# Two blocks of hybrid layers on one core: summed GLA scores, state products in alternating row halves, and a later start for GpSimd's low parts

## What is computed

```python
# first kind, twice: hybrid mixer (MLA, MOBA, retention), then a squared-ReLU MLP
x = x + hybrid_mixer(rms_norm(x, attn_norm[l]), ...)
h = rms_norm(x, mlp_norm[l])
x = x + square(relu(h @ w_mlp_up[l])) @ w_mlp_down[l]      # 1024 -> 4096 -> 1024
# second kind, twice: gated linear attention (GLA) and grouped attention side by side,
# then a gated FFN and a gated embedding
scores = where(mask, einsum(q_dec, k_intra), 0)            # per direction, chunks of 64
o = scores @ v  +  q_dec @ state
state = state * exp(last) + k_state^T @ v                  # per head, 128 x 256
o_gla = rms_norm(o_forward + o_backward)
```

## Time and profile before

| | |
|---|---|
| median of three runs | 2049.84 us |
| the profiled execution | 2049.88 us, its span 2048.1 us |
| TensorE busy, matmuls (PE) | 1942.0 us, 95% |
| VectorE busy (DVE) | 1242.6 us, 61% |
| ScalarE busy (ACT) | 998.8 us, 49% |
| GpSimd busy (POOL) | 165.7 us, 8% |
| DMA | mean 154 GB/s |

### The profile page before, as it was taken

The page is one execution under the profiler, slowest core; times in us unless marked ns, Lnnn a source line. Parts: engine busy times, 40 slices in busy tenths (PEclk is TensorE's granted clock), DMA queues, the critical chain, the costliest instruction groups (busy, mean ns, idle before and its releaser), DMA issues.

```text
span 2048.1 us, 24920 instructions
## 1 busy us (share of the span) xinstructions
PE 1942.0 (95%) x9157; PEld 1582.7 (77%) x9157; DVE 1242.6 (61%) x2017; ACT 998.8 (49%) x1510; POOL 165.7 (8%) x68
## 2 busy tenths in 40 slices
PE   7899989999999989999999999999889999999996
PEld 6777878888777778887777787888767777878885
DVE  6756664547756674546668566665575685666645
ACT  5445544444445544444543745554446347454543
POOL 0000038300000038400000000000000000000000
PEclk9999999999999999999999999999989999999998
DMA  6443555555444554554533344646434343545562
GB/s 225 126 132 114 175 165 164 185 185 179 138 124 116 182 176 152 183 178 139 179 130 106 119 148 150 193 150 216 154 117 143 119 124 124 164 151 181 178 201 72
DMA packets 167328, 315.20 MB, mean 154 GB/s; under 512 B 12180, under 2 KB 20070, under 8 KB 167080
## 3 DMA queue, kind: packets, MB, share of 16 engines
q1 hardware_dynamic: 166612, 311.87, 48.3%
q10 hardware_dynamic: 596, 1.73, 0.2%
HBM read 312.51 MB, written 1.05 MB: 153 GB/s over the span
## 4 chain that ended last, share of the span: by engine, by line
PE 85%; DVE 8%; ACT 3%; issue 2%; DMA 0%; ACTq 0%; DVEq 0%
PE acc L541 73%; PE mix L513 4%; PE mix L569 2%; DVE lo L1264 1%; PE mix L550 1%; PE mix L770 1%; PE mix L699 1%; ACT junk L988 1%; PE mix L741 1%; PE mix L737 1%; PE mix L728 1%; DVE x L1347 1%; ACT hi L944 1%; PE mix L760 1%; PE mix L557 0%
## 5 line engine op out<-in xcount | busy, mean ns | idle before, releaser
L944 ACT ACTIVATE hi<-raw 128x1024 fp32r<-128x1024 f32 x600 | 634.6, 1061 | 649.3 <-PE acc L541 606.7
L1264 DVE TENSOR_TENSOR lo<-raw,hi 128x1024 fp32r<-128x1024 f32 x536 | 646.7, 1225 | 240.4 <-ACT hi L944 225.4
L541 PE MATMUL acc<-hi,xTh 128*128 128x512 f32 (+3 forms) x1760 | 704.0, 400 | 31.7 <-DVE xTl L1294 11.9
L541 PE MATMUL acc<-lo,xTh 128*128 128x512 f32 (+3 forms) x1760 | 686.2, 390 | 0.0
L541 PE MATMUL acc<-hi,xTl 128*128 128x512 f32 (+3 forms) x1760 | 686.0, 390 | 0.0
L541 PEld LDWEIGHTS acc<-hi,xTh 128*128 128x128 f32 x1760 | 339.8, 193 | 111.8 <-issue 31.4
L541 PEld LDWEIGHTS acc<-hi,xTl 128*128 128x128 f32 x1760 | 339.2, 193 | 68.2
L541 PEld LDWEIGHTS acc<-lo,xTh 128*128 128x128 f32 x1760 | 340.7, 194 | 61.7
L917 POOL TENSOR_TENSOR lo<-raw,hi 128x1024 fp32r<-128x1024 f32 x64 | 165.5, 2611 | 677.8 <-ACT hi L944 677.8
L541 PE MATMUL acc<-hi,hTh 128*128 128x512 f32 x432 | 171.8, 398 | 0.0
L541 PE MATMUL acc<-hi,hTl 128*128 128x512 f32 x432 | 171.2, 396 | 0.0
(11 more groups left out here) (208 smaller groups left out, 1673.6 us busy)
## 6 DMA issues: line engine op xcount, KB each, us to landing
raw<-in_w_in SPq DMA_DIRECT2D x200, 512.0 KB, 3.6
raw<-in_w_ffn_in SPq DMA_DIRECT2D x80, 512.0 KB, 4.5
raw<-in_w_mlp_up SPq DMA_DIRECT2D x64, 512.0 KB, 3.6
raw<-in_w_mlp_down SPq DMA_DIRECT2D x64, 512.0 KB, 4.2
raw<-in_w_ffn_out SPq DMA_DIRECT2D x44, 512.0 KB, 4.4
raw<-in_w_out SPq DMA_DIRECT2D x32, 512.0 KB, 4.2
raw<-in_w_o_gla SPq DMA_DIRECT2D x16, 512.0 KB, 3.6
raw<-in_w_o_attn SPq DMA_DIRECT2D x16, 512.0 KB, 3.7
```

Of the source, the lines that this page charges most:

```text
L541: last = nc.tensor.matmul(out, a[:, t * P:(t + 1) * P], w[:, slot, part, 0:c.n], start=(k == 0 and a is ah and w is L.hi), stop=(k == c.k_ ...
L944: nc.scalar.activation(L.hi[:, slot], L.raw[:, slot], ACT.Copy).then_inc(*n.up("hi_ready"))
L1264: v.tensor_tensor(L.lo[:, slot], L.raw[:, slot], L.hi[:, slot].bitcast(F32), ALU.subtract).then_inc(*n.up("low_by_dve"))
```

## The change

Three edits, and the table of signal totals that goes with them. First, VectorE adds the two masked scores of a head, and TensorE makes one product with the values where there were two. Second, the six state products of a head are issued in pairs from two banks, one in partitions 0 to 63 and one in 64 to 127; the waits for both banks of a pair come ahead of it. Third, GpSimd writes `lo` for `up` chunks from `to` = 8 on only. With them, VectorE advances its stream by one unit between `head_roots` and the last `head_rope`, and by one more ahead of the wait for the GLA squares.

```diff
@@ Plan.__init__
-            by = "low_by_pool" if c.name == "up" else "low_by_dve"
+            by = "low_by_pool" if c.name == "up" and c.to >= 8 else "low_by_dve"
@@ gla_head, on TensorE
-            for i, pairs in enumerate(KV_BANKS):
-                def kv(b):
-                    for m, (d, c) in enumerate(pairs):
+            for first in (0, 2):
+                two = [L.banks.get((ln, "gla", "kv", h, i)) for i in (first, first + 1)]
+                for b, use in two:
+                    pe.wait_ge(*n.at(f"bank{b}_drained", use))
+                for m in range(len(KV_BANKS[first])):
+                    for (b, use), pairs in zip(two, KV_BANKS[first:first + 2]):
+                        d, c = pairs[m]
                         r = slice(GLA_CHUNK * (c % 2), GLA_CHUNK * (c % 2 + 1))
-                        yield nc.tensor.matmul(L.mix[:, b, m * GLA_V:(m + 1) * GLA_V], L.ks[r, d, c // 2, h * P:(h + 1) * P], gv(r, c // 2), **f32)
-                fill(("gla", "kv", h, i), kv)
+                        last = nc.tensor.matmul(L.mix[:, b, m * GLA_V:(m + 1) * GLA_V], L.ks[r, d, c // 2, h * P:(h + 1) * P], gv(r, c // 2), **f32)
+                        if m == len(pairs) - 1:
+                            last.then_inc(*n.up(f"bank{b}_filled"))
...
-                    for d in range(2):
-                        yield nc.tensor.matmul(o, L.seenT[:, h % 2, d, t, :], gv(slice(0, P), t), start=(d == 0), stop=False)
+                    yield nc.tensor.matmul(o, L.seenT[:, h % 2, 0, t, :], gv(slice(0, P), t), start=True, stop=False)
@@ second_layer, on VectorE
             drain(last, key)
+            link(v.tensor_tensor(L.seenT[:, h % 2, 0], L.seenT[:, h % 2, 0], L.seenT[:, h % 2, 1], ALU.add))
             gla_states(h)
...
         head_roots()
+        s.on(1)
         for t in range(NT):
             head_rope(8, 10, t)
         tell("params_free")
         tell("tmp_free")
         tell("rows_ready")
-        s.to(44)
+        s.to(45)
```

More of the change, by code:

```diff
@@ L205 @@
     'glu_ready'           : [18, 0, 0],
-    'dve_step'            : [400, 0, 0],
+    'dve_step'            : [408, 0, 0],
     'params_loaded'       : [8, 0, 0],
@@ L225 @@
     'scale_ready'         : [2, 0, 0],
-    'low_by_pool'         : [64, 0, 0],
-    'low_by_dve'          : [536, 0, 0],
+    'low_by_pool'         : [48, 0, 0],
+    'low_by_dve'          : [552, 0, 0],
     'ones_ready'          : [2, 0, 0],
```

## The result

The changed kernel takes 2021.74 us (median of four runs, 2020.30 to 2022.62), the kernel before 2049.22 (four runs, 2048.13 to 2050.93). The ratio is 0.9867, interval 0.9855 to 0.9879: 27.5 us faster, where the forecast of 2021 meant 28.8. The profiled execution took 2020.30 us, its span 2018.5.

A forecast was written before the change was run, and what follows sets the result against it. TensorE, busy 95% of the span, was taken as the bound; 2049.9 - 15.1 - 10.0 - 4.4 = 2020.4, with 0.4 for `rows_ready` 2020.8, said as 2021. Forecast 2016 to 2025 (0.73), range 2014 to 2030 (some 0.87).

The forecast's parts named there:

- Place one: Ahead of local unit 80, both layers of the first kind: TensorE's waits for `xTl` go whole, -15.1 us (7.74 + 7.40).
- Rival (d): Norm's long tiny operations have another cause than GpSimd; place one costs 4.5 us more a layer, 2044.5 us; chance 0.03.
- The forecast of the eight low parts: Low parts moved to VectorE around the norm, 1.22 us each, delay no unit; smallest slack 0.7 us; at worst 9.8 a layer.
- rival (a): One moved low part comes late after all, the 0.7 us slack being thin; 2024 to 2031 us; chance 0.12.
- Place two: Ahead of local unit 45, both layers of the second kind: TensorE's wait for `lo` goes, -10.0 us (5.50 + 4.50).
- The feared wait for `rows_ready`: Behind local unit 45, the later turning makes TensorE wait 0.0 to 0.2 us at worst; 0.4 allowed in all.
- The sum of the scores: One product with the values per tile in heads 0 to 3: -2.2 us a layer, -4.4 over two layers.
- Its +0.12 there: Head 3: VectorE's added sum lengthens TensorE's existing wait for a low part by 0.12 us a layer.
- The alternating products: State products in eight heads: already run in pairs, so alternating the banks wins 0; ends +8 and -2 us.
- Rival (b): Alternating spoils the state products' pairs, as each pair waits for both banks first; 2029 us (+8); chance 0.05.
- (c): The old order of state products was strict and the pairs are new; 2011 us (-10); chance 0.03.
- Rival (e): VectorE is the bound in these stretches, so added operations lengthen the path by 23.1 us; 2073 us; chance 0.04.

The follow-up runs named there:

- Experiment 7: Changed kernel with GpSimd again writing the low parts of local units 80 to 83 of the first kind: 2035.79 us, ratio 0.9933.
- Experiment 8: Kernel before, GpSimd untouched, with the norm behind the second split instead of ahead of it: 2035.65 us, ratio 0.9933.
- experiment 5: Changed kernel with each bank's wait right ahead of its first state product, products still alternating: 2021.68 us in a single run.
- experiment 4: Kernel before with the alternating order of the state products alone: 2047.95 us, ratio 0.9993.
- experiment 6: Kernel before with all state products of partitions 0 to 63 first, then all of 64 to 127: 2050.99 us in a single run.
- experiment 10: Changed kernel with the old state-product order and VectorE's stream advanced one unit ahead of the turning in head 3, not behind it: 2021.74 us.
- experiments 1 and 3: Kernel before with GpSimd writing low parts only from the third up chunk on, 2035.98 us; kernel before with the sum of the scores alone, 2042.83 us.
- the four parts alone: Kernel before with one part each: GpSimd's low parts 2035.98 us, step between roots and turning 2038.90, sum of scores 2042.83, alternating products 2047.95.
- 11: Changed kernel with the old state-product order and the attention heads' turning spread over GLA heads 1 to 3: 2014.98 us, ratio 0.9834.

## Why the prediction was right

**Place one.** Right to 0.01 us. Its ground, that GpSimd's operation holds VectorE's tiny ones, was an inference from lengths that agreed (2.37 and 2.26 to 2.32). Experiment 7 shows it: up to the second split VectorE's program is that of the changed kernel, GpSimd alone has work beside it again, and the ends agree to 0.01 us. Rival (d) falls. The forecast of the eight low parts held. In the profile after, unit 79's is done at 290.2 and due at 291.2; unit 80's, the first of four from 291.71, is done at 292.9 and due at 293.9. The slack is 1.0 us at both where I had 0.9 and 0.7, so rival (a) did not come. Experiment 8 adds what the prediction did not say: the fault was as much the order, since the split did not need the norm.

**Place two.** Right: -9.8 us against -10.0. The feared wait for `rows_ready`, put at 0.4 for two layers, did not come.

**The sum of the scores.** 4.9 us measured, 4.4 forecast: heads 0 and 1 as worked out, head 2 a little more (0.71 and 0.73 for 0.6), and in head 3 the 0.85 went into the wait as the prediction had it. Its +0.12 there did not show in the changed kernel.

**The alternating products.** That alternating by itself wins nothing holds: with the waits placed as before, both orders take 1.54 us (experiment 5). The term of 0 was wrong by a little, and the step behind it was "that wait ends as the fifth would start". It does not: the wait holds the load for the fifth product, 0.10 us a head, 0.9 us in all eight by the steps, and experiment 5 takes that away by moving the wait alone. Rival (b), lost pairs, would have given 2.56 in place of 1.64; (c), a strict order before, is refuted by experiment 4, which brought no 10 us.

The rule of the Trainium skill ("TensorE: Matmul & The Clock Gate", Part 3, "The mechanism"), that matmuls start in program order, does not hold here for products in different halves: the other half's first record passes three earlier ones (experiment 6). The price of 10.2 us that the prediction gave the rule is too high. Neighbours of two halves could overlap in program order too: by an estimate at 0.213 a step, nine steps or 1.92 us for the order before, seven or 1.49 for the alternating one, both without the start and the tail of 0.26; alternating would then win 3.4 us in eight heads. Measured is 1.54 for both orders, under the 1.92 and with no difference between them.

**Rival (e)**, VectorE as the bound, is wrong for places one and two. It is right for the stretch from head 3 on (experiment 10), where it cost 2 us a layer and not the 23 of the rival.

**The rest.** 28.8 us were forecast, 29.6 lie between the two profiled executions, 27.5 between the medians. The two misses on single terms, 0.5 more from the scores and 0.9 lost by alternating, have opposite signs, so that the sum is closer than its parts: that much is luck. The mean granted clock rose from 0.974 to 0.978, but it falls and rises at places of its own (experiments 1 and 3), worth 1 to 3 us of 2020; that is the error that a sum of removed waits keeps here. The medians of the four parts alone fell by 12.8, 9.9, 6.0 and 0.9 us. Their sum, 29.6, proves little, since the 0.9 is within the noise and has the opposite sign of what the trace shows.

## What to carry to other kernels

When tiny operations of one engine last as long as an operation of another engine beside them, and are short in its pauses, suspect that the second holds up the first, and read the busy time of the first as partly waiting. Then ask two things: whether the second engine's work can move elsewhere, and whether what stands behind the slow chain in the queue needs it at all; each of the two alone brought the whole gain here. A wait that an in-order engine causes in a stretch without idle time only moves when its work is reordered; it goes when the work is moved to where the engine idles (experiments 10 and 11).

## What the runs showed of the hardware

- One GpSimd TENSOR_TENSOR on SBUF (2.38 us for 128x1024) holds VectorE's operations on SBUF alone until it ends, however small: 2.25 to 2.35 for 128x2 in place of 0.16, 3.33 for a low part in place of 1.22. It doesn't hold those that read an operand in PSUM (1.66 for four splits, with GpSimd and without). The Trainium skill ("SBUF — State Buffer", "SBUF: two separate sides") says that the pair of ports shared by the two is locked for a whole instruction; it names VectorE's operations with two SBUF inputs, or in a mode that uses two ports, as the ones concerned. The trace agrees on the lock's length. L1306 and L1307, TENSOR_SCALAR on two int32 elements with one SBUF input, were held as well, 2.32 and 2.25 (experiment 8); in which mode they ran no run here shows.
- TensorE starts fp32 products of 64 rows ahead of earlier ones in the other half of its rows, ahead of three records in the two orders of experiment 6. Twelve records take 1.54 us when four of one half come first, and 2.03 when six do (experiment 6).
- A wait ahead of the fifth of the six state products in place of the sixth costs 0.10 us a head (experiments 4 and 5).
- The same instructions behind the same wait run at 2.4 GHz in one kernel and for the most part at 1.2 GHz in another (windows of experiments 1 and 3); what decides it these runs don't show.
